# A list scheduler on the host is told of activation-table switches and of latency between engines

## The reference, cut to what matters

```
hn   = rmsnorm(h) * norm1_w
q, k, v, g, z, xbc, dt_raw = split(hn @ w_in)          # 7184 columns
# retention, 8 heads of 128
q, k = rope(q), rope(k)
o    = (q k^T * decay) v  +  q_dec @ S ;   S = gamma^C * S + k_dec^T v
y_r  = o * rsqrt(mean(o^2 per head)) * ret_norm_w * silu(g)
# state-space mixer, 16 heads of 64, 4 groups, state 128
x, B, C = silu(causal_conv4(xbc) + conv_b)
dt   = softplus(dt_raw + dt_bias);  a_cs = cumsum(dt * -exp(a_log))
L    = exp(a_cs_i - a_cs_j) below the diagonal, 0 above
y    = (C B^T * L) (x dt)  +  (C @ H) exp(a_cs)  +  x * d_skip ;   H = exp(a_end) H + B^T (x dt exp(a_end - a_cs))
y_s  = group_rmsnorm(y * silu(z)) * ssd_norm_w
h    = h + [y_r, y_s] @ w_out
h    = h + relu(rmsnorm(h) @ w_ff1)^2 @ w_ff2
out  = rmsnorm(h) * final_norm_w
```

## Time and profile before

| | |
|---|---|
| median of the runs | 4749.06 us (2 runs, 4745.04 to 4753.08) |
| profiled execution, its own time | 4752.35 us |
| its span, slowest core (3) | 4750.8 us; the other cores 4715.2 to 4739.9 us |
| busy in the span | PE 76%, PEld 51%, DVE 44%, ACT 44%, POOL 17% |
| mean granted TensorE clock, core 3 | 0.889 |
| stage R, full tiles | 461 to 1366 us |
| stage S, light tiles | 1427 to 1899 us |
| stage S, full tiles | 1899 to 3650 us |
| stage C | 3717 to 4751 us |

### The profile page before, as it was taken

How to read it: one execution, slowest core, us unless ns; L and a number is a source line. 1 busy time by engine, 2 the same in 40 slices (tenths; PEclk the granted TensorE clock), 3 DMA queues, 4 the chain that set the end, 5 groups by cost and what they waited for, 6 DMA issues and landing times.

```text
span 4750.8 us, 90181 instructions; the slowest of 8 cores (4715.2 to 4750.8 us)
## 1 busy us (share of the span) xinstructions
PE 3592.3 (76%) x34108; PEld 2413.5 (51%) x34108; DVE 2079.5 (44%) x3589; ACT 2089.0 (44%) x3764; POOL 821.5 (17%) x1158
## 2 busy tenths in 40 slices
PE   3777788777738888776677767777774499999998
PEld 1333444433317777544444545444453377776766
DVE  3888777777765666333333333334332011111111
ACT  2333444444427777555454555455543122222222
POOL 0000000000010111222222222222223123223222
PEclk9999878888869999888788888888887799999999
DMA  6211111011043111000000100100011711111110
GB/s 130 56 52 54 33 36 34 33 36 34 24 91 79 48 51 34 23 29 25 26 25 25 37 25 27 33 29 26 25 35 42 128 37 37 37 37 37 37 37 28
DMA packets 76317, 198.92 MB, mean 42 GB/s; under 512 B 8432, under 2 KB 25328, under 8 KB 75888
## 3 DMA queue, kind: packets, MB, share of 16 engines
q1 hardware_dynamic: 62064, 157.47, 10.4%
q0 software_dynamic: 13824, 35.69, 4.6%
HBM read 185.56 MB, written 43.25 MB: 48 GB/s over the span
## 4 chain that ended last, share of the span: by engine, by line
PE 41%; DVE 24%; ACT 13%; issue 12%; DMA 4%; POOL 3%; another core or an unknown queue 1%; DVEq 1%; ACTq 0%; SPq 0%; POOLq 0%
PE ps_all L997 10%; PE ps_all L1011 10%; PE ps_all L789 6%; PE ps_all L954 6%; ACT arena L864 4%; PE ps_all L528 3%; PE ps_all L806 2%; DVE arena L875 2%; DMA xt<-xin 2%; DVE arena L505 2%; DVE arena L670 2%; DVE arena L566 2%; DVE arena L570 2%; DVE arena L565 2%; DVE arena L564 2%
## 5 line engine op out<-in xcount | busy, mean ns | idle before, releaser
L528 PE MATMUL ps_all<-arena,hnT 128*128 128x512 bf16 (+1 forms) x4224 | 956.0, 385 | 176.5 <-DMA arena<-w_in 90.7
L528 PEld LDWEIGHTS ps_all<-arena,hnT 128*128 128x128 bf16 x4224 | 404.1, 105 | 684.3 <-issue 344.7
L789 PE MATMUL ps_all<-hnT,arena 128*128 128x128 bf16 x7424 | 522.9, 237 | 120.8 <-ACT arena L756 73.5
L789 PEld LDWEIGHTS ps_all<-hnT,arena 128*128 128x128 bf16 x7424 | 492.9, 107 | 149.1 <-issue 141.3
L997 PE MATMUL ps_all<-arena 128*128 128x128 bf16 x8448 | 483.6, 219 | 96.2 <-DMA arena<-w_ff 48.5
L997 PEld LDWEIGHTS ps_all<-arena 128*128 128x128 bf16 x8448 | 476.3, 98 | 108.6 <-issue 101.1
L1011 PE MATMUL ps_all<-arena 128*128 128x512 bf16 x2112 | 465.4, 381 | 24.6 <-DMA arena<-w_ff 22.6
L1003 POOL TENSOR_TENSOR arena<-arena 128x512 bf16<-128x512 bf16 x264 | 293.7, 1112 | 747.1 <-PE ps_all L1011 536.2
L1011 PEld LDWEIGHTS ps_all<-arena 128*128 128x128 bf16 x2112 | 206.3, 98 | 269.4 <-issue 30.4
L806 PE MATMUL ps_all<-arena 128*128 128x128 bf16 x3712 | 285.9, 219 | 72.3 <-POOL arena L796 69.4
L794 ACT ACTIVATE arena<-ps_all 128x512 bf16<-128x512 f32 x232 | 138.2, 596 | 451.3 <-PE ps_all L789 449.7
(11 more groups left out here) (128 smaller groups left out, 5701.9 us busy)
## 6 DMA issues: line engine op xcount, KB each, us to landing
xt<-xin SPq DMA_DIRECT2D x132, 512.0 KB, 4.2
ax<-aux SPq DMA_DIRECT2D x132, 130.0 KB, 2.1
hmid_scr<-arena SPq DMA_DIRECT2D x33, 512.0 KB, 3.8
arena<-hmid_scr SPq DMA_DIRECT2D x33, 512.0 KB, 3.8
out<-arena SPq DMA_DIRECT2D x33, 512.0 KB, 2.8
arena<-w_in POOLq DMA_DIRECT2D x24, 512.0 KB, 35.7
yrT_scr<-arena SPq DMA_DIRECT2D x33, 256.0 KB, 2.0
arena<-yrT_scr SPq DMA_DIRECT2D x33, 256.0 KB, 2.6
```

The source lines that it names most:

```text
L528: ins = e.matmul(pb[:, 0:ncols], lhsT=hnT[:, kc, :], rhs=w3[:, kc, col0:col0 + ncols], start=(kc == 0), stop=(kc == 7))
L789: ins = e.matmul(pb[:, j * T:(j + 1) * T], lhsT=wS[:, kc, c0:c0 + T], rhs=hnT[:, kc, :], start=(kc == 0), stop=(kc == 7), skip_group_check ...
```

## The change

Two things are added to the scheduler's play-through, and none to what a tile computes. First, each ACT operation gets a class: 1 for `Exp` and `Ln`, 2 for `Silu`, 0 for the rest. When the operation that ACT would take next is of the other class than the last one with a class, the scheduler looks through the twelve earliest ready ones for one of class 0 or of the present class, recorded less than 200 operations later, and takes that one first; a switch that is made costs 1.3 us in the play-through. Second, a result is held to be ready for another engine 0.3 us after it ends.

```diff
--- before.py
+++ after.py
@@ -34,7 +34,7 @@
 
 
 class Op:
-    __slots__ = ("eng", "fn", "deps", "dma", "lane", "signal", "sem", "val", "idx", "cost", "marker", "t0", "desc")
+    __slots__ = ("eng", "fn", "deps", "dma", "lane", "signal", "sem", "val", "idx", "cost", "marker", "t0", "desc", "acls")
 
 
 class _Dummy:
@@ -58,6 +58,18 @@
     for d_ in ap.shape[1:]:
         n *= d_
     return n
+
+
+def _act_class(fn):
+    p = _Probe()
+    fn(p)
+    for name, a, k in p.calls:
+        f = k.get("func")
+        if f in (AF.Exp, AF.Ln):
+            return 1
+        if f == AF.Silu:
+            return 2
+    return 0
 
 
 def _probe_cost(eng, fn, dma):
@@ -103,8 +115,11 @@
         op = Op()
         op.eng, op.fn, op.dma, op.lane = eng, fn, dma, lane
         op.marker = False
+        op.acls = 0
         if cost is None:
             cost = _probe_cost(eng, fn, dma)
+            if eng == "act":
+                op.acls = _act_class(fn)
         op.cost = cost
         op.t0 = 0.0
         op.desc = ""
@@ -174,6 +189,7 @@
             if ndeps[id(o)] == 0:
                 heapq.heappush(future[o.eng], (0.0, o.idx, o))
         order = []
+        act_cls = [0]
         n_left = len(seg)
         while n_left:
             best = None
@@ -191,7 +207,23 @@
                 rt, idx, o = heapq.heappop(future[e])
                 heapq.heappush(avail[e], (idx, rt, o))
             idx, rt, o = heapq.heappop(avail[e])
+            if e == "act" and o.acls and o.acls != act_cls[0] and avail[e]:
+                cand = sorted(avail[e])[:12]
+                alt = None
+                for c in cand:
+                    if c[2].acls in (0, act_cls[0]) and c[0] - idx < 200:
+                        alt = c
+                        break
+                if alt is not None:
+                    avail[e].remove(alt)
+                    heapq.heapify(avail[e])
+                    heapq.heappush(avail[e], (idx, rt, o))
+                    idx, rt, o = alt
             start = max(t, rt)
+            if e == "act" and o.acls:
+                if o.acls != act_cls[0]:
+                    start += 1.3
+                act_cls[0] = o.acls
             if o.dma:
                 free[e] = start + 0.06
                 fin = start + o.cost
@@ -204,7 +236,7 @@
             n_left -= 1
             for u in users.get(id(o), ()):
                 ndeps[id(u)] -= 1
-                r = max(ready_t.get(id(u), 0.0), fin)
+                r = max(ready_t.get(id(u), 0.0), fin + (0.0 if u.eng == o.eng else 0.3))
                 ready_t[id(u)] = r
                 if ndeps[id(u)] == 0:
                     heapq.heappush(future[u.eng], (r, u.idx, u))
```

## The result

The changed kernel takes 4977.5 us (median of 11 runs), against 4739.6 to 4753.1 for the undisturbed runs of the kernel before: a ratio of 1.0487, 95% interval 1.0474 to 1.0501.

The account below looks back on a forecast made before the run. Stage S's full part was taken as bound by a chain of waits between engines. 198 (handover) + 0 + 22 (stage R) = 220 us on 4752.35 gave 4972, less 3.3 over the median 4969, taken as 4970; range 4865 to 5050.

Parts of the forecast that it names:

- The handover: Between stage S full tiles: exps end 6.1 us earlier, late Silu delays DVE; 6.2 us a tile longer, 198 us.
- E to Z: From output projection L954's end to the next tile's first projection L528: 28.7 us before, 35 us forecast.
- the DVE row: DVE work in one row behind the late Silu, from four products L875 to copy L505: 11.0 us, then 0.14 to PE.
- Z to L954: From the next tile's first projection L528 to its output projection L954: 16.5 us before, taken as unchanged, 0.
- the rival that it wins time back: Y path on POOL or PE's clock returns 2.4 to 3.6 us a tile: 4854 us, chance 0.12.
- L954, also taken as unchanged: Stage S output projection, left as it was on the whole; bounds -1.5 and +1.3 us a tile.
- Stage R, +22 us: Stage R's full tiles: L687 starts later behind four rope steps; 0.7 us a tile longer, 22 us.
- The hole: Stage R: L687's 1.99 us wait for an exp behind a table load, to be filled by four rope steps.
- the moved L670: Stage R: two L670 now ahead of L640 delay the output's square by less than rope's slack: 0.
- side figure for a projection at full clock: Stage R: with the first projection block at full clock (1.8 us), a gain of about 0.45 a tile, -14 us.
- The loads: Table loads: 331 in both orders, no saving; one leaves the handover, one comes new ahead of small exp L761.
- The drain: Rival: the skill's 1.38 us drain per switch is real, 2.8 us a tile more, near 5060 us, chance 0.02.

Follow-up runs that it names:

- Without loads: Kernel before with Relu in place of Silu in stages R and S, orders kept, all table loads but one gone: ratio to kernel before 0.9487.
- the look-ahead: Kernel before with only ACT's look-ahead past the other table class added to the scheduler, no switch price, no latency: fastest 4803.8 us against 4739.6.
- Undoing one of two moves: Changed kernel, stage S full-tile handovers: last Silu, copies, convolution and transposes put back on ACT and PE, fastest 4975.75 us; or DVE's order put back, ratio 1.0708.
- undoing both: Changed kernel with the ACT and PE step and DVE's order both put back in stage S's full-tile handovers: ratio to the kernel before 1.0282.
- another order: Kernel before with stage S alone scheduled otherwise, by trace costs and searched priority shifts for some lines: fastest 4649.4 us, ratio 0.9803.
- the run without loads: Changed kernel with Relu in place of Silu in stages R and S, orders kept: ratio to the kernel before 0.9908, fastest 4683.6 us.

## Why the prediction was right, point by point

**The handover.** The walk gave 6.2 us a tile and 198 us; E to Z grew by 6.06, 194 us. Its steps, as times after E, forecast and then measured in the handover above: the last exp 18.1, 18.6; the last Silu's end 21.7, 22.1; the first product 23.7, 24.2; Z 34.8, 34.0. Two pieces of the walk missed by a little, in opposite directions. Ahead of the exps the prediction said that nothing that matters moves and counted two loads between E and Z. There are three: the first Silu L851 has one of its own at 2689.95, because what ran last ahead of E is now the exps (the norm's and three small ones), behind both Silus of z; before, the second Silu of z ran last. The first exp starts 0.76 us later in the mean (E + 11.33, before 10.57). And the DVE row was costed at 11.1 us and took 9.8: seven of its operations (the ones behind L907, L868, L907, L931, L960, L935 and the last L960) start about 0.19 us closer to the one ahead than costed, 0.60 us for a size of 512 columns and not 0.80.

**Z to L954, taken as 0.** It is 16.80 against 16.57, and by the cores with all records 16.5 against 16.6: nothing. In the handover above, POOL's last L943 ended at 2723.13, Z + 4.6 (forecast 4.0), and the sixteen z matmuls at Z + 6.7, as forecast:

```profile
2720.15 5.01 PE L560 MATMUL ps_all<-arena,hnT 128*128 128x512 bf16 x15 [1.31 <-DVE arena L931]
...
2721.98 1.15 POOL L943 TENSOR_TENSOR arena<-arena 128x512 f32<-128x512 f32 x1
...
2727.39 1.29 ACT L788 ACTIVATE arena<-ps_all 128x512 bf16<-128x512 f32 x2
```

The y path was ready first and had to wait for the Silus L788; the rival that it wins time back falls.

**L954, also taken as unchanged, wasn't.** With all 32 records it takes 9.2 us in the changed kernel. Against the 8.43 of core 3 that is 0.8 a tile, some 25 us and within the bounds of the prediction; core for core it is 0.8 to 1.7, past its upper bound of 1.3 on four of the six cores with all records in both traces. It goes with the granted clock during L954: 0.85 on core 3 and 0.90 to 0.95 on the others before, 0.76 to 0.78 on all now. That the forecast of the total wasn't hurt more is luck: the slowest core, which makes the metric, was the one whose L954 was slow already.

**Stage R, +22 us, was mis-sized.** Measured alone it is 3 us, -3 to +10. From one start of L712 to the next it is 27.52 us, from one L680 to the next 27.36 before. The hole is filled as forecast:

```profile
824.09 0.42 DVE L596 TENSOR_TENSOR arena<-ps_all,ax 128x256 f32<-128x256 f32 x1 [1.95 <-PE ps_all L560]
...
825.68 0.42 DVE L600 TENSOR_TENSOR arena<-ps_all,ax 128x256 f32<-128x256 f32 x1
826.02 1.48 DVE L719 TENSOR_TENSOR arena<-ps_all,arena 128x512 f32<-128x512 f32 x2
```

but two terms of the prediction were off. It costed the four rope steps alike in both orders. In the kernel before, behind the earlier trace rows, they took longer, with a wait for each other:

```profile
820.54 0.42 DVE L564 TENSOR_TENSOR arena<-ps_all,ax 128x256 f32<-128x256 f32 x1
...
822.47 0.43 DVE L568 TENSOR_TENSOR arena<-ps_all,ax 128x256 f32<-128x256 f32 x1 [0.46 <-DVE arena L566]
```

From L564 to the end of L568 are 2.36 us, from L596 to the end of L600 2.01, and L719 starts beside the last. And it put the moved L670 at nothing, since rope gives the square slack. The views of DVE's waits in the full tiles of stage R say otherwise, the first line before, the others now:

```profile
DVE arena L687 <- ACT arena L684: 65.6, 33, 2.0
...
DVE arena L712 <- ACT junk L710: 38.8, 33, 2.4
DVE arena L596 <- PE ps_all L560: 28.8, 36, 2.1
```

The wait of 2.0 us a tile for the exp is gone. In its place DVE waits 1.2 us a tile for the square ahead of L712, which it didn't before, and 0.9 for the projection ahead of rope: 65.6 us against 67.6. So one wait was traded for two that come to the same. The prediction's side figure for a projection at full clock, a gain of 0.45 a tile, doesn't follow from its own rows either: they give about 1.1 (L687 at 818.8 against 819.9).

**The loads.** All groups together have 329 loads, as before. The new one stands ahead of L793, whose group has grown to 64, from 33 at L761:

```profile
L793 ACT ACT_TABLE_LOAD x64 | 82.1, 1283 | 70.4 <-DVE arena L791 69.8
```

The drain that the Trainium skill states ("ScalarE: Activation LUTs", What ACT_TABLE_LOAD costs) doesn't show: L549 ends at 2704.66, the load runs from 2704.67 to 2705.95, and the Silu starts at 2705.97. Without loads E to Z of the kernel before is 4.15 us shorter, 1.38 for each of three loads, where a load itself is 1.28. By the Trainium skill's 2.66 a switch my estimate for the three would be 8.0. The Trainium skill's rule on the same page (Rules for kernel authors), to do all of one set before switching, wasn't worth anything here: the look-ahead, with 64 loads fewer, was 1.4% slower.

**The sum.** 4970 forecast, 4977.5 measured: 220 us against some 231 between the ratio's two sides. The mechanism came out as forecast: 194 us between E and Z, where 198 stood. That the totals lie so close is in part luck, since what was put at 0 (L954 and the pieces around the handovers, some 27 us) made up for stage R, 3 to 5 us where 22 stood.

## What to carry to other kernels

Before an order of work is changed, ask of each long piece on one engine what the other engines do meanwhile, and whether it still can be done there. Bringing the long piece forward is worth nothing if the small operation that feeds the others now stands behind it. Undoing one of two moves gave nothing or cost 2% more, undoing both gave 2%: such moves have to be undone as a pair too. A play-through with a wrong delay (0.3 us everywhere, where the earlier trace rows have 0.10 from the last exp to the first product and 0.14 from the copy to PE) can do more harm than one without any; no run tried 0.1. The number of table loads is no measure of an order: with 265 the kernel was 1.4% slower than with 329, with 333 in another order 2% faster.

## What the runs showed of the hardware

DVE operations of 128x512 that needn't wait for the one just ahead start 0.60 us apart, though each is counted at 0.68 (2713.93, 2714.53, 2715.13, 2715.73), so their ends overlap. Where the kernel has recorded a dependence on the one just ahead, the start is 0.79 after it: L956 at 2715.73 and L960 at 2716.52, which reads what L956 wrote, but also the four L875 of the earlier trace rows, four in 3.07 us, which write separate parts of one buffer. The trace shows a semaphore wait on DVE's own count ahead of each of those. So what goes with the 0.19 us seems to be the wait and not the data; no run took such a wait away. A list of durations alone misses this.

The granted clock differs with the order of work: in the full part of stage S it is 0.84 in the kernel before and 0.76 in the changed one, where PE is busy 62% of the time and no longer 71%. The same 32 matmuls of L954 go with the clock granted while they run: 7.07 us in tiles at 1.0, 8.7 at 0.81, 9.9 at 0.71. The mean over the stretch doesn't tell which it will be: in the run without loads the changed order has 0.80 in that part, under the kernel before with its loads, and every L954 of it ran at 1.0.
